# Spreading the running gate sums over the partitions by way of DRAM instead of TensorE, in a two-layer hybrid block

## The reference

```python
g = jnp.cumsum(g.reshape(b, h, n, c), axis=-1)
decay = jnp.exp(jnp.where(incl, g[..., :, None] - g[..., None, :], -jnp.inf))
lower = jnp.where(strict, jnp.einsum('bhnid,bhnjd->bhnij', k_beta, k) * decay, 0.0)
t_inv = lax.linalg.triangular_solve(lower + eye, jnp.broadcast_to(eye, lower.shape),
                                    left_side=True, lower=True, unit_diagonal=True)
...
attn = jnp.einsum('bhnid,bhnjd->bhnij', q, k) * decay
```

## Time and profile before

| | |
|---|---|
| median of three runs | 904.03 us (903.77 to 905.48) |
| the profiled execution, its own time | 905.12 us |
| its span from first to last instruction | 903.1 us |
| TensorE matmul busy | 893.1 us (99%) |
| TensorE weight load busy | 761.2 us (84%) |
| VectorE busy | 669.1 us (74%) |
| ScalarE busy | 513.9 us (57%) |
| GpSimd busy | 2.4 us |
| mean busy share of the 16 DMA engines, queue of SyncE | 62.8% |
| granted clock of TensorE, mean | 0.997 of full speed |

### The profile page before, as it was taken

One profiled execution on the slowest core, in us unless ns is written; L12 is line 12 of the kernel. 1 busy time (PEld: TensorE's weight loads), 2 busy tenths in 40 slices (PEclk: granted clock), 3 DMA queues, 4 the chain that ended last, 5 costly groups with the idle time before them and its releaser, 6 DMA issues.

```text
span 903.1 us, 13837 instructions
## 1 busy us (share of the span) xinstructions
PE 893.1 (99%) x5410; PEld 761.2 (84%) x5410; DVE 669.1 (74%) x1107; ACT 513.9 (57%) x877; POOL 2.4 (0%) x6
## 2 busy tenths in 40 slices
PE   9999999999999999999999999999999999999997
PEld 5999898888887888888889998988888888888885
DVE  6869887778968666656778798767988675665656
ACT  6586556785446544444565866568744554444444
POOL 0000000000000000000000000000000000000000
PEclk9999999999999999999999999999999999999998
DMA  8645646657664777678655374486667467768671
GB/s 294 205 167 164 202 127 180 238 201 230 200 234 153 219 198 251 213 211 261 214 181 175 119 213 155 126 236 229 209 203 237 149 213 221 250 188 259 219 205 46
DMA packets 129056, 180.55 MB, mean 200 GB/s; under 512 B 82272, under 2 KB 88160, under 8 KB 128992
## 3 DMA queue, kind: packets, MB, share of 16 engines
q1 hardware_dynamic: 128560, 179.34, 62.8%
q10 hardware_dynamic: 432, 0.34, 0.1%
HBM read 169.16 MB, written 10.49 MB: 199 GB/s over the span
## 4 chain that ended last, share of the span: by engine, by line
PE 93%; DVE 5%; ACT 1%; issue 0%; ACTq 0%; DVEq 0%
PE bank L620 8%; PE bank L622 7%; PE bank L621 7%; PE bank L492 7%; PE bank L494 7%; PE bank L493 7%; PE bank L697 6%; PE bank L395 5%; PE bank L434 5%; PE bank L436 5%; PE bank L435 5%; PE bank L396 5%; PE bank L397 5%; PE bank L424 2%; PE bank L423 2%; PE bank L422 2%
## 5 line engine op out<-in xcount | busy, mean ns | idle before, releaser
L938 ACT CAST whi<-raw 128x1024 fp32r<-128x1024 f32 x290 | 303.6, 1053 | 296.3 <-PE bank L494 94.5
L1288 DVE TENSOR_TENSOR wlo<-raw,whi 128x1024 fp32r<-128x1024 f32 x290 | 347.6, 1216 | 66.7 <-ACT whi L938 64.1
L395 PE MATMUL bank<-ahi,whi 128*128 128x256 f32 x448 | 129.6, 289 | 0.8 <-DVE tmp L1338 0.8
L396 PE MATMUL bank<-alo,whi 128*128 128x256 f32 x448 | 126.7, 283 | 0.0
L397 PE MATMUL bank<-ahi,wlo 128*128 128x256 f32 x448 | 126.6, 283 | 0.0
L620 PE MATMUL bank<-whi,ahi 128*128 128x512 f32 x288 | 114.8, 399 | 0.6 <-DVE alo L1352 0.5
L622 PE MATMUL bank<-whi,alo 128*128 128x512 f32 x288 | 112.4, 390 | 0.0
L621 PE MATMUL bank<-wlo,ahi 128*128 128x512 f32 x288 | 112.3, 390 | 0.0
L492 PE MATMUL bank<-whi,ahi 128*128 128x512 f32 x288 | 112.2, 390 | 0.0
L494 PE MATMUL bank<-whi,alo 128*128 128x512 f32 x288 | 112.1, 389 | 0.0
L493 PE MATMUL bank<-wlo,ahi 128*128 128x512 f32 x288 | 112.0, 389 | 0.0
(11 more groups left out here) (299 smaller groups left out, 1305.8 us busy)
## 6 DMA issues: line engine op xcount, KB each, us to landing
raw<-stream_dram SPq DMA_DIRECT2D x292, 512.0 KB, 4.7
turned_dram<-proj SPq DMA_DIRECT2D x144, 32.0 KB, 1.7
proj<-turned_dram SPq DMA_DIRECT2D x18, 256.0 KB, 4.6
proj<-gbias_dram SPq DMA_DIRECT2D x12, 256.0 KB, 4.4
probs_dram<-proj SPq DMA_DIRECT2D x8, 192.0 KB, 4.3
proj<-probs_dram SPq DMA_DIRECT2D x2, 768.0 KB, 5.9
par<-params_dram SPq DMA_DIRECT2D x2, 556.5 KB, 6.5
x<-x_dram SPq DMA_DIRECT2D x2, 512.0 KB, 5.3
```

The lines of the kernel that those rows point to most:

```text
L395: pe.matmul(dst, whi_of(m)[:, wcol], hi, start=first, stop=False, skip_group_check=True)
L396: pe.matmul(dst, whi_of(m)[:, wcol], lo, start=False, stop=False, skip_group_check=True)
L938: act.copy(whi_of(m), raw_of(m)).then_inc(*AC.up(("hi", m), "w"))
L1288: dv.tensor_tensor(wlo_of(m), raw_of(m), whi_of(m), ALU.subtract).then_inc(*DV.up(("lo", m), "w"))
```

## The change

TensorE no longer spreads the sums. SyncE writes `gcol` (128 partitions x 8) to a new DRAM buffer `gsum` of 8 x 128 numbers, 4 KB, so that each 4-byte number lands in a place of its own, waits for that, and reads the 4 KB back into `E1` on each of the 128 partitions (512 KB on the way in). ScalarE makes the differences in place in `E1`, two steps later than before, and takes the exponential two steps later too. TensorE's "kk", which uses the same banks 4 and 5, no longer waits for the differences.

```diff
@@ SyncE
+                    if k == 15:
+                        sp.wait_ge(*DV.at(l, "gcol"))
+                        sp.dma_start(gsum.rearrange("g q -> q g"), sm["gcol"], allow_slow_non_contiguous=True).then_inc(written_g, 16)
+                    if k == 16:
+                        sp.wait_ge(written_g, 16 * (l + 1))
+                        sp.dma_start(flat(tiles(E1, 4)), gsum.rearrange("g q -> (g q)").unsqueeze(0).broadcast_to([P, 8 * P])).then_inc(loaded_g, 16)
@@ TensorE, side(l, k)
-                if k == 11:
-                    pe.wait_ge(*DV.at(l, "gcol"))
-                    pe.wait_ge(*DV.at(l, ("zs", 1)))
-                    for g in range(8):
-                        ins = turn(4, g, sm["gcol"][:, g:g + 1].broadcast_to([P, P]))
-                    ins.then_inc(*PE.up("gbc"))
...
                 if k == 15:
-                    pe.wait_ge(*AC.at(l, "dif"))
+                    pe.wait_ge(*DV.at(l, ("zs", 1)))
@@ ScalarE, side(l, k)
-                if k == 12:
-                    act.wait_ge(*PE.at(l, "gbc"))
+                if k == 14:
+                    act.wait_ge(loaded_g, 16 * (l + 1))
                     for g in range(8):
-                        act.activation(wide(E1, 4)[:, g, :], b3(4 + g // 4, 4)[:, g % 4, :], ACT.Identity, bias=sm["gneg"][:, g:g + 1]).then_inc(*AC.up("dif"))
+                        act.activation(wide(E1, 4)[:, g, :], wide(E1, 4)[:, g, :], ACT.Identity, bias=sm["gneg"][:, g:g + 1]).then_inc(*AC.up("dif"))
                     act.activation(sm["egc"], sm["gcol"], ACT.Exp).then_inc(*AC.up())
-                if k == 13:
+                if k == 15:
                     act.wait_ge(*PO.at(l, "causal"))
                     act.activation(wide(E1, 4), wide(E1, 4), ACT.Exp).then_inc(*AC.up("decays"))
```

More of the change, by code:

```diff
@@ L97, in last, with build @@
         return self.sem, self.n - back
-def build(nc, wstream, params, gbias, consts, norms, final, x_in, ident_in, ab_in, mixture, turned, probs, vturn, qturn, out, known):
+def build(nc, wstream, params, gbias, consts, norms, final, x_in, ident_in, ab_in, mixture, turned, probs, vturn, qturn, gsum, out, known):
     ctx = ExitStack()
@@ L143, in build @@
         written_hid, loaded_hid = sem("written_hid"), sem("loaded_hid")
+        written_g, loaded_g = sem("written_g"), sem("loaded_g")
         written_v, loaded_v = sem("written_v"), sem("loaded_v")
@@ L1992 @@
         args.append(nc.dram_tensor("qturn_dram", (4, 32, 8 * P), F32, kind="Internal").ap())
+        args.append(nc.dram_tensor("gsum_dram", (8, P), F32, kind="Internal").ap())
         o = nc.dram_tensor("out_dram", (P, 2, D), F32, kind="ExternalOutput").ap()
```

## The result

The changed kernel takes 916.09 us, the median of four runs (915.78 to 917.83), beside 904.75 us (903.77 to 905.83) for the kernel before on the same chip: a ratio of 1.013, 95% interval 1.0115 to 1.0145. The forecast of 901.7 us and its range (900.4 to 904.8) were wrong, and in sign: the case that came true is the rival in which the sums land too late, beyond the time given to it (906.9). The profiled execution took 915.87 us, with a span of 914.1 us against 903.1, so 11.0 us more, and a mean granted clock of 0.990 against 0.997.

What follows compares the result with a forecast made beforehand. TensorE's work plus two stalls bound the kernel; 1.73 us a layer was possible, VectorE allowed 1.16, so 1.16 x 2 = 2.3 us took the median from 904.0 to 901.7, range 900.4 to 904.8.

Steps and rivals of the forecast that it cites:

- the rival in which the sums land too late: ScalarE idles before the differences, delaying VectorE and TensorE; slower if landing passes 61.2 us, 906.9 at 62.6; chance 0.13.
- What bounds the kernel: TensorE's list of work, 99% busy, plus its stalls, traced back to a crowded ScalarE at 52 to 60 us.
- The two stalls: TensorE before "X 0" for the convolution, 0.46 us, and before "X 1" for level 1, 0.39: 0.85 a layer.
- What is removed: Eight transposes on TensorE, costing 0.88 us a layer with nothing hidden.
- the sum of 2.3: Whole-kernel gain: VectorE lets TensorE be 1.16 us earlier in each of two layers, below TensorE's possible 1.73.
- The write of 3.7 us: SyncE's write of 1,024 4-byte pieces, issued at 50.1 us, done at 53.8; rows allowed 1.7 to 4.1.
- The read of 4.7 us: Read into all partitions takes a weight load's median, landing at 58.5 us, 1.1 before ScalarE asks at 59.57.
- ScalarE and VectorE worked forward: Third convolution 1.81 us earlier; GpSimd's masking delays L1565 by 0.65, leaving L1580 1.16 earlier.
- the rival "only the transposes": Something unseen keeps VectorE where it is relative to TensorE; only 1.8 us gained, 902.3; chance 0.06.
- The price of lateness: Late sums stall ScalarE, then VectorE before L1580, then TensorE before "X 0" and "X 1"; at 62.6 loses 1.4 a layer.
- the formula: Sums landing x us after 59.57 give a gain of 1.6 - x a layer, through a later "decay" before L1580.
- Signs named in advance: Prediction is wrong if ScalarE idles before the differences, the write exceeds 6 us, or VectorE waits for "decay".

Runs made afterwards that it cites:

- the kernel before with another order: Kernel before, VectorE's two rotary products and four rotary sums moved one step earlier, ahead of the third convolution; 902.29 us, ratio 0.9980.
- 32-byte pieces: Changed kernel, 4 KB written unturned as 128 pieces, values in wrong places, exponential scaled by 0.001; 901.91 us, ratio 0.9977.
- blocks: Changed kernel, sums turned in 32 x 32 blocks by one VectorE instruction and written as 32 pieces of 128 bytes; 902.32 us, ratio 0.9979.
- only the differences later: Kernel before, ScalarE's differences and exponential two steps later, TensorE still spreading the sums, no transfer; 904.09 us, ratio 0.9999.
- the run with blocks and the new order: Changed kernel, sums turned in 32 x 32 blocks on VectorE, rotary products and sums ahead of the third convolution; 901.16 us, ratio 0.9968.

## Why the prediction was wrong

**What bounds the kernel: right.** The two stalls and their 0.85 us a layer were real; the kernel before with another order gains 1.9 us, and 1.7 was worked out.

**What is removed: right.** With sums that came in time the change gained 2.2 us (32-byte pieces) and 1.9 (blocks), against the sum of 2.3; 1.8 of it are the transposes. The trace of after shows them by themselves: from the two matmuls of "gcum" to the key transposes TensorE took 6.84 us before (47.95 to 54.79) and takes 5.97 after (47.30 to 53.27), 0.87 less, where 0.88 were forecast.

**The write of 3.7 us: this is the step that failed.** It took 10.4 us in the first layer and 10.2 in the second (497.39 to the read's issue at 507.54), 6.5 to 6.7 more than taken. I had bounded it by writes of 1,024 and 256 pieces and called the count of pieces and the queue what sets the time. All those pieces are of 128 bytes. The runs show that the queue doesn't do it here, and the count only by a small part, but 4-byte pieces that are neighbours in DRAM: 8.4 to 10.6 us on an empty queue, against 2.4 to 3.5 for as many with one in 64 or 512 bytes and 2.1 for as many of 32 bytes. Why neighbours are dear stays open. The bound above, 4.1 us, was no bound for an operation of another kind, and the range was too narrow by it.

The Trainium skill ("DMA: Bandwidth & Descriptors", rules for kernel authors) warned against a transpose by a rearranged access pattern. The direction of that rule is borne out here: the same 4 KB took 9.5 us turned and 1.4 us not turned, a factor of 7. Its factor of 19 is against the hardware's own DMA transpose, which no run here has, so it is neither borne out nor refuted.

**The read of 4.7 us: right.** 4.99 us in the first layer, 5.4 in the median of both.

**ScalarE and VectorE worked forward: right in kind, GpSimd too cheap.** Counted from `hi(15)`, with the difference to before in brackets:

| | third convolution | L1580 |
|---|---|---|
| before (48.21) | 12.43 | 21.90 |
| 32-byte pieces (47.30) | 10.53 (-1.90) | 20.90 (-1.00) |
| blocks alone (47.47) | 10.54 (-1.89) | 20.91 (-0.99) |
| only the differences later (47.73) | 11.39 (-1.04) | 21.77 (-0.13) |

The forecast had the convolution 1.81 us earlier and L1580 1.16. Between them lies GpSimd: 0.65 us forecast, 0.90 measured. One half of it came as forecast: GpSimd's instruction is itself held until `lo(18)` is over. But the prediction let the first two instructions of `kb` pass, since they have one input, and had L1565 wait; with 32-byte pieces it is the first of them that was held. (The Trainium skill, "SBUF — State Buffer", Who interferes with whom, lists the operations that can take the shared port pair, and has `tensor_scalar` among them; I had used only its rule on two inputs. The 1.07 us for 0.17 agree with the list.) Which one is held depends on who comes first. In the run with blocks and the new order GpSimd starts at 61.33, just as `lo(18)` ends; L1561 and the reciprocal behind it take their 0.16 and 0.20 us, and L1565 takes 0.70 instead of 0.17, as the prediction had it. A layer gains what VectorE gains, 1.0 us, and TensorE keeps both its stalls: its weight loads stand 0.41 us for the convolution and 0.51 for level 1 with 32-byte pieces, against 0.53 and 0.53. The forecast had VectorE 1.16 us earlier, which by its own sum leaves about 0.1 of the convolution's stall; that it would go was wrong. So the rival "only the transposes" (902.3) describes the sum as well as the forecast does: the later differences give 1.0 us a layer and GpSimd takes 0.9.

**The price of lateness: half right.** In the count of before the sums landed at 65.47, 5.9 us after ScalarE could take them, and in the second layer ScalarE stood 6.6 us for them. By the formula, 1.6 - x, the layers would lose 4.3 and 5.0. The loads of "X 1" give 5.65 and 5.72, and without the 2.0 and 1.4 us of the clock 3.7 and 4.3, some 0.6 less than the formula. L1581 itself is 3.7 us late in the first layer (73.19 - 47.56 = 25.63 against 21.90). Half of these 0.6 is the 0.3 us that the prediction had put on the path of "decay" for GpSimd, which in the changed kernel ran in a gap of VectorE (67.53) and held nobody up there. The size is near, the way was another: TensorE didn't stand before "X 0" and "X 1" for L1580 and the levels, but at half-chunk 18 for the copy at L1101, at the end of ScalarE's own queue. What the formula had not at all is the lower clock behind the pause. So the rival's 906.9, which reached only to a landing at 62.6, becomes 916 by two things: the landing was later still (3 us in the first layer), and the clock took 3.4 us more.

**Signs named in advance.** Of the three that would make the prediction wrong, all came: ScalarE idles before the differences (5.85 us), the write takes over 6 us (10.4), and VectorE waits for "decay" (1.19 us before L1581 at 73.19).

## What to carry to other kernels

Before a turn or a spread is given to a DMA write, look at the size of its pieces and where they land: 4-byte pieces next to each other cost 6.6 to 10.6 us here, for 128 as for 1,024 of them, so turn on an engine first (one VectorE instruction in blocks of 32) and let the DMA write whole runs and broadcast on the read, which took no longer than a plain read of the same size. A latency that is hidden by 1 us of margin is bounded by rows of the same kind or not at all. If no row has its kind of piece, start the transfer earlier by the size of the doubt, as the order of the engines allows. A wait put into an in-order queue is priced by everything behind it there, and when TensorE stands still for some microseconds, by the slower clock behind it as well.

## What the runs showed of the hardware

- Writes of 4-byte pieces that are neighbours in DRAM took 8.4 to 10.6 us for 1,024, 8.1 for 512, 7.6 for 256 and 6.7 for 128, on an empty queue; spread to one in 32 bytes or more, 2.4 to 3.5 us for 1,024. In both runs the first such write took 2 us longer than the second (10.4 and 10.6 against 8.4). The values for one in 32 and one in 64 bytes (3.0 and 3.5) stand the wrong way round, so differences of 0.5 us mean little.
- A read of one 4 KB stretch by all 128 partitions (512 KB) took 3.7 us, as a read of 512 KB of weights beside it.
- GpSimd's masking of a 128 x 1024 tile held back a VectorE instruction with a single input of 128 x 8 numbers for 0.9 us, and itself took 1.6 to 2.1 us instead of 1.09 where it started beside a VectorE instruction with two inputs (`lo`). A reciprocal of 128 x 8 numbers took its usual 0.20 us beside it.
- In a pause of 5.15 us of TensorE the granted clock fell to 1.2 GHz, and behind it matmuls came at 0.22 us each instead of 0.12, for 4.6 us; in one of 5.86 us it fell too, and the slow matmuls lasted 3.1 us. Behind a pause of 3.10 us they began only 1.2 us after work had resumed (74.8 against 73.6); behind one of 2.2 us there were none.
